# Two reorderings in a two-block transformer kernel: the next query's norm products ahead of an even head's third score tile, and one weight split between two copies

## What is computed

```
fq, fk, fv, f_logit, sq, sk, sv, g_fox, g_sb = split_columns(h @ w_in)
fq = rms_norm(fq.reshape(b, s_len, 8, 64), q_norm)     # per head
fk = rms_norm(fk.reshape(b, s_len, 8, 64), k_norm)
...
q = (rms_norm_2(c_q, g_cq) @ w_uq).reshape(B, L, 8, 96)
k = concatenate([k_nope, k_r])
q = rms_norm_2(q, g_qn)                                 # the query's norm: a mean of squares per token
k = rms_norm_2(k, g_kn)
q, k = rotary on the last 32 columns
s = einsum('bqhd,bkhd->bhqk', q, k) * scale
p = softmax(s)
attn = einsum('bhqk,bkhd->bqhd', p, v)
```

## Time and profile before

| | us |
|---|---|
| median of 3 runs | 1693.21 (1693.07 to 1694.72) |
| the profiled execution's own time | 1693.01 |
| its span, first to last instruction | 1690.9 |
| PE busy | 1676.6 (99% of the span) |
| DVE busy | 1026.4 (61%) |
| POOL busy | 716.1 (42%) |
| ACT busy | 639.2 (38%) |

### The profile page before, as it was taken

The page is one execution under the profiler, slowest core; times in us unless marked ns, Lnnn a source line. Parts: engine busy times, 40 slices in busy tenths (PEclk is TensorE's granted clock), DMA queues, the critical chain, the costliest instruction groups (busy, mean ns, idle before and its releaser), DMA issues.

```text
span 1690.9 us, 21138 instructions
## 1 busy us (share of the span) xinstructions
PE 1676.6 (99%) x7666; PEld 1369.4 (81%) x7666; DVE 1026.4 (61%) x1216; ACT 639.2 (38%) x895; POOL 716.1 (42%) x303
## 2 busy tenths in 40 slices
PE   9999999999999999999999999999999999999999
PEld 7887888887788887888888888888777668888887
DVE  6767566527665446357675566785564753969451
ACT  5222222235665656222322222213546754343321
POOL 3444344434333421344444344443455433444443
PEclk9999999999999999999999999999999999999999
DMA  5332233325211221243423323332252023233243
GB/s 194 102 109 90 79 100 100 107 80 194 88 63 58 93 75 38 76 136 100 139 90 110 101 88 100 101 102 94 90 187 75 26 100 125 88 100 100 94 142 113
DMA packets 42815, 171.04 MB, mean 101 GB/s; under 512 B 4937, under 2 KB 5065, under 8 KB 41452
## 3 DMA queue, kind: packets, MB, share of 16 engines
q1 hardware_dynamic: 38736, 148.13, 27.0%
q10 hardware_dynamic: 3996, 21.73, 3.7%
HBM read 159.22 MB, written 10.62 MB: 100 GB/s over the span
## 4 chain that ended last, share of the span: by engine, by line
PE 68%; issue 22%; POOL 6%; DVE 2%; ACT 1%; DMA 0%; POOLq 0%; SPq 0%; DVEq 0%; ACTq 0%
PE psum L307 20%; PE psum L309 20%; PE psum L308 20%; POOL wlo L273 6%; PE psum L1201 1%; PE psum L1758 1%; PE psum L1735 1%; PE psum L752 1%; PE psum L737 0%; PE psum L1191 0%; PE psum L1219 0%; DMA raw<-wk_dram 0%; PE psum L723 0%; DVE psum L445 0%; ACT mprob L1913 0%
## 5 line engine op out<-in xcount | busy, mean ns | idle before, releaser
L273 POOL TENSOR_TENSOR wlo<-raw,whi 128x1024 fp32r<-128x1024 f32 (+2 forms) x258 | 663.7, 2573 | 887.7 <-ACT whi L295 887.1
L295 ACT ACTIVATE whi<-raw 128x1024 fp32r<-128x1024 f32 (+2 forms) x259 | 286.1, 1105 | 704.7 <-PE psum L309 694.8
L307 PE MATMUL psum<-h_hi,whi 128*128 128x512 f32 x1360 | 536.9, 395 | 2.5 <-POOL wlo L273 1.6
L309 PE MATMUL psum<-h_hi,wlo 128*128 128x512 f32 x1360 | 529.7, 389 | 0.0
L308 PE MATMUL psum<-h_lo,whi 128*128 128x512 f32 x1360 | 529.5, 389 | 0.0
L307 PEld LDWEIGHTS psum<-h_hi,whi 128*128 128x128 f32 x1360 | 255.4, 188 | 63.6 <-POOL wlo L273 4.5
L308 PEld LDWEIGHTS psum<-h_lo,whi 128*128 128x128 f32 x1360 | 255.5, 188 | 53.6 <-issue 2.2
L309 PEld LDWEIGHTS psum<-h_hi,wlo 128*128 128x128 f32 x1360 | 255.3, 188 | 53.3
L307 PE MATMUL psum<-mid_hi,whi 128*128 128x512 f32 x352 | 137.2, 390 | 0.0
L309 PE MATMUL psum<-mid_hi,wlo 128*128 128x512 f32 x352 | 137.0, 389 | 0.0
L308 PE MATMUL psum<-mid_lo,whi 128*128 128x512 f32 x352 | 136.9, 389 | 0.0
(11 more groups left out here) (387 smaller groups left out, 2383.5 us busy)
## 6 DMA issues: line engine op xcount, KB each, us to landing
raw<-wk_dram SPq DMA_DIRECT2D x220, 512.0 KB, 3.5
raw<-wd_dram SPq DMA_DIRECT2D x32, 704.0 KB, 4.1
raw<-wp_dram SPq DMA_DIRECT2D x8, 640.0 KB, 3.9
x_scratch<-xT ACTq DMA_DIRECT2D x2, 2048.0 KB, 8.9
spectra_scratch<-spec_out ACTq DMA_DIRECT2D x4, 1024.0 KB, 5.8
xT<-x_scratch ACTq DMA_DIRECT2D x8, 512.0 KB, 4.7
spec<-spectra_scratch ACTq DMA_DIRECT2D x2, 2048.0 KB, 10.2
xT<-x_dram SPq DMA_DIRECT2D x4, 512.0 KB, 7.7
```

Source lines behind the costliest of these rows:

```text
L273: pool.tensor_tensor(wlo[s][:, 0:w], raw[s][:, 0:w], whi[s][:, 0:w].bitcast(F32), ALU.subtract).then_inc(lo_ready, 1)
L295: act.activation(whi[s][:, 0:w], raw[s][:, 0:w], ACT.Copy).then_inc(hi_ready, 1)
L307: pe.matmul(dst, s_hi, m_hi, start=start and i == 0, stop=False, **kw)
L309: last = pe.matmul(dst, s_lo, m_hi, start=False, stop=stop and i == n - 1, **kw)
```

## The change

In ACT's loop of the forget projections, between the two copies of i = 0, all units up to `unit(2) + 1` are split. That is one unit, the second of `fox_k`; its split stood behind the second copy. In the latent attention, the norm products of head h + 1 move from behind to ahead of the third score tile for h = 2, 4 and 6; for h = 0 and the odd heads they stay where they are. No instruction is added or taken away.

```
@@ -980,6 +980,8 @@
                         src, dst = stage32[i % 2], fq_both if i < 4 else fk_hi
                         for e in range(2):
                             act.activation(dst[main[e], 2 * (i % 4) + e, :], src[main[e], :], ACT.Copy).then_inc(self.hi, 1)
+                            if i == 0 and e == 0:
+                                split_hi_to(act, self.unit(2) + 2)
                         if j == 2:
                             split_hi_to(act, BASE["fox_k"] + 2)
                         if i == 2:
@@ -1780,8 +1782,10 @@
                         self.tensor_turn(pe, h - 1, 2)
                     else:
                         self.tensor_v(pe, 2)
+                    if h and h % 2 == 0:
+                        self.tensor_query_sum(pe, h + 1)
                     self.tensor_scores(pe, h, 2)
-                    if h + 1 < HEADS:
+                    if h == 0 or h % 2 and h + 1 < HEADS:
                         self.tensor_query_sum(pe, h + 1)
                     if h:
                         self.tensor_turn(pe, h - 1, 3)
```

## The result

The changed kernel takes 1699.87 us in the median of six runs (1698.19 to 1701.54), the kernel before on the same chip 1693.31 (1693.07 to 1694.98): a ratio of **1.0034 [1.0024, 1.0044]**, 0.34% slower, where 0.13% faster was forecast. The two medians lie 6.6 us apart. The profiled execution of the changed kernel took 1698.21 us, its span 1696.1 against 1690.9 before.

The account below looks back on a forecast made before the run. PE, busy 99% of the span, was taken to bound the kernel; 1.62 us from the latent attention plus 0.66 from the forget projections made 2.28, from 1693.21 to 1690.9 us, range 1689.8 to 1692.8.

Parts of the forecast that it names:

- PE bounds the kernel, and only its idle time can be won: Whole kernel: PE is busy 99% of the span; no instruction is removed, so only PE's idle time can be won.
- The hole in the latent attention: PE's 0.70 us idle before tile 2 in head 2; norm products fill it, gaining 0.54 us in each of three heads.
- the spare 0.17: Latent attention, new wait of some 0.17 us before tile 3, which would first absorb a slow handover to the norm products.
- the slower rival that I priced: Heads 3, 5, 7: norm products push tile 2 and delay the next head's first turn; 1693.8 us, chance 0.03.
- The split: Forget projections: the split moves ahead of one copy, so PE starts the fourth unit 0.66 us earlier, at 412.36.
- The bounds 0.41 to 0.76: Forget projections: PE's gain in us from the split if POOL's instruction takes 2.75 or 2.40 us.
- DVE held by POOL at i = 0: Forget projections: i = 0's low parts run into POOL; the scaling of i = 1 starts at about 416.25 instead of 415.82.
- DVE's delay at i = 0 priced at nothing: Forget projections: the sixth unit is ready by 422.5, PE wants it at 424.4; 1.9 us of slack, cost nothing.
- Slower than 1696.6 has no mechanism that I can price: Whole kernel: the outcome slower than 1696.6 us, chance 0.02.
- the rivals that give back the split: Only the latent part counts: DVE holds the split or POOL, or 0.66 us is lost later; 1691.6 us, chance 0.09.
- The spread: Whole kernel: the runs shown spread by up to 1.5 us over their lowest.

Follow-up runs that it names:

- split alone: Kernel before with only the moved split, the norm products staying in place: 1699.83 us against 1693.86, ratio 1.0036.
- two fills: Kernel before with two added DVE fills of 128x512 (0.48 us each) ahead of the scaling of i = 1: 1700.84 us against 1693.86, ratio 1.0042.
- one-fill kernel: Kernel before with one added DVE fill of 0.48 us ahead of the scaling of i = 1: 1693.98 us against 1694.60, ratio 1.0000.
- kernel with both edits and the new order: Changed kernel with DVE's casts ahead of the low parts and three side jobs moved into its wait for ACT's copies: 1690.75 us against 1694.60, ratio 0.9979.
- norm products alone: Kernel before with only the moved norm products, the split staying in place: 1693.09 us against 1693.86, ratio 0.9991.

## Why the prediction was wrong, step by step

- **PE bounds the kernel, and only its idle time can be won.** Right. It can also be lost, and what was lost is again idle time of PE.
- **The hole in the latent attention.** Right in the sum, 0.54 us a head, and in the mechanism: a new wait of 0.13 us stands ahead of tile 3 (a step of 0.49 from turn to tile 3, against 0.36). Tile 2 comes 0.18 us later than before, measured from its turn (1322.06 - 1320.82 against 1315.12 - 1314.06), where I had 0.11. The handover from a turn to the norm products, which no row showed, took 0.43 us against the 0.36 that I took; the spare 0.17 paid for it, as the text allowed. Heads 3, 5 and 7 had no new wait: the slower rival that I priced did not occur.
- **The split.** Right and a little low: 0.86 us instead of 0.66, because POOL's instruction took 2.38 us and not the 2.50 of its row, and began at 409.73 instead of 409.80. The bounds 0.41 to 0.76 were too narrow by 0.10.
- **DVE held by POOL at i = 0.** Right. The low parts took 3.03 us, the casts 2.97, and the scaling of i = 1 started at 416.40, forecast 416.25. The Trainium skill's GPSIMD Engine Reference, section Key points, names two kinds of VectorE instructions that contend with GpSimd, those "in a 2-port perf mode or with two SBUF inputs"; the prediction gave only the second. The trace agrees for the low parts, which read two SBUF inputs: the pair took 3.03 us against 1.40. The casts read one SBUF input and were held as well, 2.97 us for the pair against 0.87; whether they ran in such a mode no row says.
- **DVE's delay at i = 0 priced at nothing: "What hangs on it is ACT's two copies (to about 418.3) and, behind them, a square of 0.6, a split of 1.06 and POOL's 2.5, in all until 422.5 ... 1.9 us of slack. Cost nothing."** This is the step that failed. Its times came out: the copies ended at 418.47, POOL at 422.67, and PE did not wait there. But I asked of POOL only when it *ends*, for PE. I had just written down that DVE stretches under POOL, and did not ask when POOL *starts*, against DVE's next casts. The trace of before had it: the second cast started at about 419.84, POOL at 420.56, a margin of 0.72 us, and the change takes 416.40 - 415.85 = 0.55 of it on DVE and, through ACT's wait for an earlier PE, 420.56 - 420.26 = 0.30 on POOL, 0.85 together. And I treated the slack as that of one round, where DVE, ACT and POOL release each other in a loop: a delay that is made again in each round isn't covered by 1.9 us of slack. In place of nothing the runs showed a held cast in four rounds and PE falling back by 5.95 us, from 0.86 ahead to 5.09 behind.
- **"Slower than 1696.6 has no mechanism that I can price: 0.02."** That chance followed from the step above. All the rivals that give back the split ended at its own 0.66 us. A delay on an engine off the critical path was given no price below zero.
- **The spread.** The text took 1.5 us as the spread of the runs over their lowest; it was 1694.72 - 1693.07 = 1.65. It is a step, not a spread: some 1.6 us for a stretch of PE at half clock of 3.4 us. The sum had no term for such stretches, and they are the other 3.1 of the 6.6 us. That the new waits bring them is likely and not shown run by run: none of the 15 runs with the four held casts (changed kernel, split alone, two fills) has a mean clock of 1.000, where ten of the first 22 runs of before have, and in the traces of the split alone and of the two fills the stretch lies right at the new waits, but in that of the changed kernel it lies elsewhere.

## What to carry to other kernels

When an edit moves work by half a microsecond on an engine with slack, ask not only whether the consumer has slack, but what the moved instruction now starts beside; for DVE beside POOL, set the starts of both next to each other for the next rounds of the loop, too. Where engines release each other in a circle, one late round can lock them into a slower one: look for the wait that used to absorb it (here 0.88 us of ACT for PE). In this kernel DVE's work stood best where it fitted between POOL's instructions, and the side jobs in the gap in which DVE waits for ACT; that turned a loss of 5.1 us at the end of the forget projections into a gain of 0.9.

## What the runs showed of the hardware

- In the forget projections an instruction of DVE with all its inputs in SBUF that starts while POOL subtracts 128x1024 does not end before POOL does: two casts 0.87 us free, 2.97 to 3.01 with the second held, and that one ends 0.28 us behind POOL; a low part 0.70 free, 1.82 in the earlier trace rows, 0.55 behind POOL; the gate steps 0.69 free, 2.78 held; the scan 1.23 free, 3.31 held. POOL's own instruction took 2.38 to 2.41 us at those casts.
- Which of the two starts first decides. In the one-fill kernel a cast that started 0.1 us ahead of POOL wasn't held, and POOL took 2.59 us there. In the kernel with both edits and the new order, POOL began at 420.16, under a low part that had started at 420.03; the low part took its 0.69 us, and POOL 2.83 instead of 2.41.
- What DVE reads out of PSUM, alone or with one input in SBUF, isn't held: in the one-fill kernel, with POOL busy from 420.65 to 423.24, the addition at 421.02 took 0.75 us, and so did the scaling behind it.

```profile
421.02 0.75 DVE L1071 TENSOR_SCALAR prob<-psum,vec 128x512 f32<-128x512 f32 x1
421.86 0.75 DVE L1020 SCALAR_TENSOR_TENSOR scratch<-psum,small,scratch 128x512 f32<-128x512 f32 x1
```

- The granted clock of PE falls to 1.2 GHz for 3.4, 6.8 or 10.2 us in some executions, in these traces 0.1 to 2 us behind a wait of PE of 1.1 to 1.95 us. A stretch of 3.4 us costs 1.6 us, one of 6.8 at the stick sums 3.2 (the norm products alone, where PE is 0.05 ahead before it and 3.17 behind after it), the one of 10.2 over a wait 2.6. The same wait of 1.95 us at the stick sums stands in all eleven traces, and five of them have a stretch behind it. What decides this stays open.
- Not tried: a kernel whose low weight part runs elsewhere than on POOL, which would have taken the contention away altogether.
